# Two heads' retention scores in one run, four grouped heads' values in one run, and a different order at the start, at the first grouped head and at the end of a two-layer trunk

## The reference, cut to what matters

```python
h = x
h = h + _mixer_mla_retention(_rmsnorm(h, ab_norm[i]), ab_w_in[i], ..., ab_w_out[i])   # layer 0
h = h + _swiglu(_rmsnorm(h, ffn_norm[i]), ffn_w_gate[i], ffn_w_up[i], ffn_w_down[i])
h = h + _mixer_swa_stickbreak(_rmsnorm(h, cd_norm[i]), cd_w_in[i], swa_sinks[i], cd_w_out[i])  # layer 1
h = h + _moe(_rmsnorm(h, moe_norm[i]), moe_router[i], moe_w_gate[i], moe_w_up[i], moe_w_down[i])
return _rmsnorm(h, final_norm)

def _rmsnorm(x, g):
    y = xf * lax.rsqrt(jnp.mean(xf * xf, axis=-1, keepdims=True) + EPS)
    return (y * g.astype(jnp.float32)).astype(x.dtype)

# retention, within a block of 128 rows
inner = jnp.einsum('nbqhd,nbkhd->nbhqk', qc, kc) * decay_in[None, None]
out_inner = jnp.einsum('nbhqk,nbkhv->nbqhv', inner, vc)

# one block of the grouped heads
s = jnp.einsum('bqhgd,bkhd->bhgqk', qi, ki, ...) * scale - slopes * dist_f
s = jnp.where(valid, s, -jnp.inf)
m = jnp.maximum(jnp.max(s, axis=-1, keepdims=True), sink)
p = jnp.exp(s - m)
p = p / (jnp.sum(p, axis=-1, keepdims=True) + jnp.exp(sink - m))
return jnp.einsum('bhgqk,bkhd->bqhgd', p.astype(vi.dtype), vi)
```

## Time and profile before

| | us |
|---|---|
| median of 3 runs | 1516.37 |
| lowest and highest run | 1515.61 and 1517.12 |
| the profiled execution, its own time | 1517.4 |
| its span | 1515.5 |
| PE busy | 1501.0 (99%) |
| DVE busy | 1263.5 (83%) |
| ACT busy | 1098.7 (72%) |

### The profile page before, as it was taken

How to read it: one execution, slowest core, us unless ns; L and a number is a source line. 1 busy time by engine, 2 the same in 40 slices (tenths; PEclk the granted TensorE clock), 3 DMA queues, 4 the chain that set the end, 5 groups by cost and what they waited for, 6 DMA issues and landing times.

```text
span 1515.5 us, 22215 instructions
## 1 busy us (share of the span) xinstructions
PE 1501.0 (99%) x7294; PEld 1238.4 (82%) x7294; DVE 1263.5 (83%) x1557; ACT 1098.7 (72%) x1388; POOL 25.8 (2%) x25
## 2 busy tenths in 40 slices
PE   9999999999999999999999999999999999999997
PEld 7778888888877788888888888888888888888885
DVE  5578676666677779999999999999999999999997
ACT  6565555555567757888888788888788788788886
POOL 0000000000000000000000000000000000000000
PEclk9999999999999989999999999999999999999998
DMA  9533374555545459999999999999999999999970
GB/s 339 192 113 128 142 257 167 209 205 195 190 171 178 142 206 398 413 403 394 388 372 386 380 378 376 379 388 368 380 392 367 381 393 360 386 391 358 412 271 30
DMA packets 193224, 454.00 MB, mean 300 GB/s; under 512 B 8176, under 2 KB 12144, under 8 KB 192912
## 3 DMA queue, kind: packets, MB, share of 16 engines
q1 hardware_dynamic: 190560, 443.72, 78.1%
q0 software_dynamic: 2608, 9.57, 2.3%
HBM read 447.37 MB, written 5.90 MB: 299 GB/s over the span
## 4 chain that ended last, share of the span: by engine, by line
PE 97%; DVE 2%; ACT 1%; issue 0%; DVEq 0%; ACTq 0%
PE bank L316 26%; PE bank L318 26%; PE bank L317 26%; PE bank L1515 6%; PE bank L1518 3%; PE bank L2046 1%; PE bank L386 1%; PE bank L818 1%; PE bank L1336 0%; PE bank L1490 0%; PE bank L1327 0%; PE bank L807 0%; PE bank L1811 0%; PE bank L372 0%; DVE w_lo L329 0%; PE bank L2162 0%
## 5 line engine op out<-in xcount | busy, mean ns | idle before, releaser
L329 DVE TENSOR_TENSOR w_lo<-ring_low,w_hi 128x1024 fp32r<-128x1024 f32 (+2 forms) x442 | 532.1, 1216 | 86.8 <-ACT w_hi L325 58.5
L325 ACT ACTIVATE w_hi<-ring_low 128x1024 fp32r<-128x1024 f32 (+2 forms) x442 | 465.5, 1055 | 133.4 <-PE bank L318 126.1
L329 DVE TENSOR_TENSOR w_lo<-ring,w_hi 128x1024 fp32r<-128x1024 f32 x330 | 397.1, 1222 | 35.3 <-ACT w_hi L325 12.4
L325 ACT ACTIVATE w_hi<-ring 128x1024 fp32r<-128x1024 f32 x328 | 346.5, 1061 | 81.0 <-PE bank L318 81.0
L316 PE MATMUL bank<-w_hi,xe_hi 128*128 128x512 f32 x888 | 350.3, 395 | 0.0
L318 PE MATMUL bank<-w_hi,xe_lo 128*128 128x512 f32 x888 | 346.1, 390 | 0.0
L317 PE MATMUL bank<-w_lo,xe_hi 128*128 128x512 f32 x888 | 345.5, 389 | 0.0
L318 PEld LDWEIGHTS bank<-w_hi,xe_lo 128*128 128x128 f32 x888 | 166.7, 188 | 35.4
L317 PEld LDWEIGHTS bank<-w_lo,xe_hi 128*128 128x128 f32 x888 | 166.9, 188 | 33.1
L316 PEld LDWEIGHTS bank<-w_hi,xe_hi 128*128 128x128 f32 x888 | 166.8, 188 | 33.0
L316 PE MATMUL bank<-w_hi,hT_hi 128*128 128x512 f32 x448 | 175.8, 392 | 0.0
(11 more groups left out here) (335 smaller groups left out, 1673.2 us busy)
## 6 DMA issues: line engine op xcount, KB each, us to landing
ring<-m_gate_dram SPq DMA_DIRECT2D x72, 1024.0 KB, 5.4
ring_low<-m_down_dram SPq DMA_DIRECT2D x72, 1024.0 KB, 6.2
ring<-m_up_dram SPq DMA_DIRECT2D x56, 1024.0 KB, 5.4
ring_low<-m_up_dram SPq DMA_DIRECT2D x56, 1024.0 KB, 6.4
ring_low<-m_gate_dram SPq DMA_DIRECT2D x40, 1024.0 KB, 5.7
ring<-m_down_dram SPq DMA_DIRECT2D x40, 1024.0 KB, 6.3
ring_low<-f_gate_dram SPq DMA_DIRECT2D x14, 1024.0 KB, 5.1
ring_low<-f_up_dram SPq DMA_DIRECT2D x14, 1024.0 KB, 6.1
```

The source lines that it names most:

```text
L325: nc.scalar.activation(w_hi[:, buf, 0:width], src, ACT.Copy).then_inc(hi_ready, 1)
L329: nc.vector.tensor_tensor(w_lo[:, buf, 0:width], src, f32(w_hi[:, buf, 0:width]), ALU.subtract).then_inc(split_ready, 1)
```

## The change

Five things are changed; the arithmetic of each result stays the same.

1. **Start.** On ACT the split of unit 4 now stands ahead of the squares, and the squares and the root are spread: block 0 at d = 0, block 1 and the root at d = 1, the wait for `rstd` at d = 2. DVE's reciprocal moves from d = 0 to d = 1, behind its split of unit 4.
2. **Retention scores.** Heads 0 and 1 are issued one behind the other at d = 25, into banks 4 and 7.
3. **First grouped heads.** `scores(0)` (which computes heads 0 and 1) moves from between units 6 and 7 into the middle of unit 7. At d = 8 `exponentials(0)` and `normalised(0)` stand ahead of the split of unit 11 instead of behind it.
4. **Values.** `values` runs four heads at d = 12, 16, 20 and 24, two calls in a row, into the two halves of bank 7. There are four `pT_sb1` buffers instead of two. The mixed parts follow at d = 13, 17, 21 and 25, two pairs each: `mixed_hi(k)` at the start of the step, `mixed_hi(k+1)` behind the weight split and the exponentials, then on DVE `mixed_lo(k)` and `mixed_lo(k+1)` behind `normalised`, both waiting for `mixed_hi(k+1)`.
5. **End.** The last norm works in halves of 512 columns: ACT squares the left halves while DVE still adds the right ones, ACT scales the last block's right half with a product that DVE made ahead, and four DMAs of 256 KB take the place of two of 512 KB.

```diff
-        def sums_of_squares(act, use, by_block):
-            for tb in range(TB):
+        def sums_of_squares(act, use, by_block, blocks=range(TB)):
+            for tb in blocks:
...
+            if TB - 1 not in blocks:
+                return
...
-        def pair_out(bank, v, a):
+        def pair_out(bank, v, a, c0=0):
 
             for first in (True, False):
-                cols, src = (slice(0, 256), slice(0, 256)) if first else (slice(P, 256), slice(256, 384))
+                cols, src = (slice(c0, c0 + 256), slice(0, 256)) if first else (slice(c0 + P, c0 + 256),
+                                                                                slice(256, 384))
...
-        R_BANK = (7, 7, 7, 6, 7, 6, 7, 6)
-        RET_AT = {24: (0,), 25: (1,), 26: (2, 3), 27: (4, 5), 28: (6, 7)}
+        R_BANK = (4, 7, 7, 6, 7, 6, 7, 6)
+        RET_AT = {25: (0, 1), 26: (2, 3), 27: (4, 5), 28: (6, 7)}
...
-                if d + 3 < L0_UNITS:
+                if d + 3 < L0_UNITS and d != 1:
                     l0_hi(act, d + 3)
                 if d == 0:
-                    sums_of_squares(act, 0, False)
+                    l0_hi(act, 4)
+                    sums_of_squares(act, 0, False, (0,))
+                if d == 1:
+                    sums_of_squares(act, 0, False, (1,))
+                if d == 2:
                     act.wait_ge(rstd_done, 1)
...
-                if d == 0:
+                if d == 1:
                     inverse_rms(dve, 0)
...
-                if i:
-                    pe.wait_ge(ret_decayed, {1: 2, 2: 4, 3: 2}.get(i, 2 * i - 2))
+                if i == 0:
+                    pe.wait_ge(nm_done, MLA_H)
+                if i > 1:
+                    pe.wait_ge(ret_decayed, {2: 4, 3: 2}.get(i, 2 * i - 2))
...
             def turned_copy(i):
                 n = MLA_H + i
                 act.wait_ge(pT_banked, n + 1)
-                act.wait_ge(pv_done, n - 1)
-                nc.scalar.activation(pT_sb1[i % 2], pt_bank(i), ACT.Copy).then_inc(pT_done, 1)
+                act.wait_ge(pv_done, n - 3)
+                nc.scalar.activation(pT_sb1[i % 4], pt_bank(i), ACT.Copy).then_inc(pT_done, 1)
 
             def mixed_hi(k):
                 if k < 8:
-                    act.wait_ge(pv_done, MLA_H + 2 * k + 2)
+                    act.wait_ge(pv_done, MLA_H + 4 * (k // 2) + 4)
...
-                if d % 2 and 11 <= d <= 25:
-                    mixed_hi((d - 11) // 2)
+                if d in (13, 17, 21, 25):
+                    mixed_hi((d - 13) // 2)
+                if d == 25:
+                    mixed_hi(7)
...
+                if d == 8:
+                    exponentials(0)
                 if d + 3 < L1_UNITS and d != 1:
                     d_hi(act, d + 3)
...
-                if swa_at(d, 1) is not None and d < 21:
+                if swa_at(d, 1) is not None and 8 < d < 21:
                     exponentials(swa_at(d, 1))
+                if d in (13, 17, 21):
+                    mixed_hi((d - 13) // 2 + 1)
...
             def mixed_lo(k):
-                dve.wait_ge(mixT_hi_done, KM + k + 1)
+                dve.wait_ge(mixT_hi_done, KM + (k | 1 if k < 8 else k) + 1)
...
-                if d % 2 and 11 <= d <= 25:
-                    mixed_lo((d - 11) // 2)
+                if d == 25:
+                    mixed_lo(6)
+                    mixed_lo(7)
...
+                if d == 8:
+                    normalised(0)
                 if d in (22, 23):
                     d_lo(dve, d + 2)
...
-                if swa_at(d, 1) is not None and d < 22:
+                if swa_at(d, 1) is not None and 8 < d < 22:
                     normalised(swa_at(d, 1))
+                if d in (13, 17, 21):
+                    mixed_lo((d - 13) // 2)
+                    mixed_lo((d - 13) // 2 + 1)
...
+                    if (d, kk) == (7, 1):
+                        pe.wait_ge(cT_dve, 2)
+                        scores(0)
...
             def values(i):
                 pe.wait_ge(pT_done, MLA_H + i + 2)
-                if i:
+                if i and i % 4 == 0:
                     pe.wait_ge(mixT_done, KM + i // 2)
...
-                if d == 7:
-                    pe.wait_ge(cT_dve, 2)
...
-                if swa_at(d, 0) is not None and d % 2:
+                if swa_at(d, 0) is not None and d % 2 and d > 7:
                     scores(swa_at(d, 0))
-                if swa_at(d, 3) is not None and d % 2 == 0:
-                    values(swa_at(d, 3))
+                if d in (12, 16, 20, 24):
+                    values(d - 12)
+                    values(d - 10)
...
         def last_root(act, part):
             nc.scalar.preload_act_table(ACT.Sqrt)
             for tb in range(TB):
+                act.wait_ge(sc_done, 4 * part + 5 + tb)
+                nc.scalar.activation(squares[:, tb, :], h[:, tb, 0:512], ACT.Square,
+                                     accum_out=ss_left[:, tb:tb + 1]).then_inc(left_sq, 1)
+            for tb in range(TB):
...
                 act.wait_ge(sc_done, 4 * part + 7 + tb)
-                nc.scalar.activation(squares, h[:, tb, :], ACT.Square, accum_out=ss[:, tb:tb + 1]).then_inc(sq_done, 1)
+                nc.scalar.activation(squares[:, 2 + tb, :], h[:, tb, 512:D], ACT.Square,
+                                     accum_out=ss[:, tb:tb + 1]).then_inc(sq_done, 1)
...
+            nc.scalar.activation(xn[:, 1, 512:D], squares[:, 4, :], ACT.Copy, scale=rstd[:, 1:2]).then_inc(act_scaled, 1)
...
+            nc.vector.tensor_tensor(squares[:, 4, :], h[:, 1, right], fgain[:, right], ALU.mult).then_inc(gained, 1)
+            inverse_root(0)
+            scaled(0, left)
+            inverse_root(1)
+            scaled(0, right)
+            scaled(1, left)
...
+            sp.wait_ge(xn_done, 1)
+            store(0, 0)
+            sp.wait_ge(xn_done, 2)
+            store(0, 1)
+            sp.wait_ge(act_scaled, 1)
+            store(1, 1)
+            sp.wait_ge(xn_done, 3)
+            store(1, 0)
+            sp.wait_ge(out_done, 64)
```

More of the change, by code:

```diff
@@ L166, in trunk @@
         pT_sb1 = [place(f"pT_sb1{i}", [P, 384], at=L1_AT + 24576 + 1536 * i) for i in range(2)]
+        pT_sb1 += [place(f"pT_sb1{i + 2}", [P, 384], at=L1_AT + 37376 + 1536 * i) for i in range(2)]
         bv1 = place("bv1", [P, TB, 512], at=L1_AT + 27648)
@@ L178, in trunk @@
         hT_lo = [place(f"hT_lo{i}", [P, 4, P], F32R, at=(ARENA + 6144, XT_AT + 6144)[i]) for i in range(2)]
-        squares = place("squares", [P, D], at=XT_AT)
+        squares = place("squares", [P, 5, 512], at=XT_AT)
         g_moe_row = place("g_moe_row", [P, D], at=XT_AT + 12288)
@@ L2385, in last_root, with inverse_root, scaled @@
                                      scale=1.0 / D).then_inc(rms_done, 1)
+            act.wait_ge(gained, 1)
+            act.wait_ge(rstd_done, 6)
+            nc.scalar.activation(xn[:, 1, 512:D], squares[:, 4, :], ACT.Copy, scale=rstd[:, 1:2]).then_inc(act_scaled, 1)
         def last_norm(dve):
-            dve.wait_ge(gain_in, 16)
-            for tb in range(TB):
+            def inverse_root(tb):
                 dve.wait_ge(rms_done, 4 + tb + 1)
                 nc.vector.reciprocal(rstd[:, tb:tb + 1], rms[:, tb:tb + 1]).then_inc(rstd_done, 1)
+            def scaled(tb, w):
@@ L2392, in last_norm @@
                 dve.wait_ge(rstd_done, 4 + tb + 1)
-                nc.vector.scalar_tensor_tensor(out=xn[:, tb, :], in0=h[:, tb, :], scalar=rstd[:, tb:tb + 1],
-                                               in1=fgain, op0=ALU.mult, op1=ALU.mult).then_inc(xn_done, 1)
+                nc.vector.scalar_tensor_tensor(out=xn[:, tb, w], in0=h[:, tb, w], scalar=rstd[:, tb:tb + 1],
+                                               in1=fgain[:, w], op0=ALU.mult, op1=ALU.mult).then_inc(xn_done, 1)
+            left, right = slice(0, 512), slice(512, D)
@@ L2489, in _, with store @@
             overflow(sp, moe_sp, moe_sp(sp, 0))
-            for tb in range(TB):
-                sp.wait_ge(xn_done, tb + 1)
-                sp.dma_start(out[0, tb * P:tb * P + P, :], xn[:, tb, :]).then_inc(out_done, 16)
-            sp.wait_ge(out_done, 32)
+            def store(tb, r):
+                w = slice(512 * r, 512 * r + 512)
+                sp.dma_start(out[0, tb * P:tb * P + P, w], xn[:, tb, w]).then_inc(out_done, 16)
+            sp.wait_ge(xn_done, 1)
[7 more added lines that the diff above has]
+            sp.wait_ge(out_done, 64)
         @block.scalar
```

16 lines of the change are left out of this document (13 added, 3 removed).

## The result

| | us |
|---|---|
| kernel before, median of 15 runs | 1516.54 (1515.61 to 1517.70) |
| changed kernel, median of 15 runs | 1520.66 (1518.54 to 1522.28) |
| ratio, 95% interval | 1.0026, 1.0020 to 1.0033 |
| profiled execution of the changed kernel, its span | 1522.11, 1520.3 |

The changed kernel is 4.1 slower (with the interval, 3.0 to 5.0). The page of its profile says as little as that of before: PE is still 99% busy.

What follows compares the result with a forecast made beforehand. PE was taken as the bound (busy 1501.0 of 1515.5), with a 4.03 ACT and DVE chain in grouped-head steps. Gains -2.75, costs +5.7 and clock +1.7 gave +4.65 on 1516.37: 1521.0 us, range 1517.2 to 1522.8.

Steps and rivals of the forecast that it cites:

- start: At the kernel's start, unit 4's earlier split removes PE's 0.53 idle and the refilling of its pipe: -0.75 us.
- retention: At d = 25, retention heads 0 and 1 overlap in different banks, so one head's scores are free: -0.9 us.
- first grouped head: At the first grouped heads, p_sb is ready earlier and the first transpose no longer waits: -0.4 us (0 to -0.45).
- values, steps: At d = 12, 16, 20 second values runs lengthen PE's list; steps losing a run gain nothing: +2.05 us.
- values, d = 24: At d = 24, where PE is already dense, the values run moved there costs its full 0.65 us.
- values, gap at d = 21 and 22: mixed_lo, waiting for the second mixed_hi, delays s_sb on DVE; PE idles 3.9 before transpose 14: +3.0 us (2.6 to 3.3).
- clock behind the gap: After PE's 3.9 gap the clock falls to half speed for some time: +1.7 us, between 0 and 4.
- end: After PE's last matmul, the last norm in halves shortens the path: -0.7 us (-0.2 to -1.2).
- Rival B: The gap comes, but the clock doesn't fall or comes back at once: +2.95, 1519.3 us; chance 0.20.
- Rival D: No gap, and steps at d = 12, 16, 20 absorb the second run: some -3.4, 1513.0 us; chance 0.09.
- C: The gap doesn't come, as mixed_hi or mixed_lo is released earlier than read: 1516.3 us; chance 0.12.
- E: Clock stays low as long as at 546, or the d = 22 delay spreads: +6.5 to +8, 1523 to 1524.5; chance 0.08.

Runs made afterwards that it cites:

- e3: The changed kernel with 18 extra matmuls, results unread, on PE in the gap ahead of transpose 14: 1519.22 us, 2.55 above before.
- e1: The changed kernel with the second mixed_hi of d = 21 moved on ACT ahead of the split of unit 24: 1516.39 us, ratio 1.000.
- e4: The kernel before with the fourth part (values) alone: 1524.28 us, ratio 1.0057.
- e5: The changed kernel with the fourth part (values) undone: 1513.53 us, ratio 0.9981 to before.
- e9b: e5 with two extra matmuls on PE ahead of the wait for x's second half: 1512.99 us, ratio 0.9977 to before.
- e12b: e5 run once more, unchanged, on the same chip as e9b: 1513.73 us, ratio 0.9984 to before.
- e6: e1 with both mixed_lo of d = 21 ahead of normalised(13), and exponentials and normalised ahead of the splits at d = 10, 14, 18: 1514.18 us, ratio 0.9981.
- e7: The kernel before with the first part (start) alone: 1516.69 us, ratio 0.9995.
- e8: e5 with one wait more, retention head 1 waiting until head 0's scores are banked: 1515.65 us, one execution only.

## Why the prediction was right

It gave 1521.0 with 1517.2 to 1522.8 and slower by over 0.2%; the median is 1520.66, +4.1 against the +4.65 of the sum. Term by term, as the prediction put it:

| term | forecast | measured | from |
|---|---|---|---|
| start | -0.75 (-0.4 to -0.8) | -0.9 to -1.1 | 17.54 to 17.76 against 18.68, where the clock stayed up |
| retention | -0.9 | -1.04 | the table of stretches |
| first grouped head | -0.4 | -0.42 | the same |
| values, steps | +2.05 | +1.78 | transpose 0 to 13 |
| values, d = 24 | +0.65 | +0.65 | transpose 15 to the transposes of h |
| values, gap at d = 21 and 22 | +3.0 | +2.96 | transpose 13 to 14 |
| clock behind the gap | +1.7 | +1.65 | transpose 14 to 15, and e3 |
| end | -0.7 | -0.58 | last matmul to the end (in all profiles: 8.1 to 8.6 with the new end, 8.9 to 9.5 with the old) |

With -1.0 for the start the measured terms add up to +4.0, and the medians differ by 4.1.

**The gap** was read from the order of two engines and timed with rows of the kernel before, and this is the term that carried the forecast. Each link of it stands in the timeline above: `mixed_hi` behind the split (forecast for 493.12; transpose 13 comes 1.0 later in this execution, and `mixed_hi` at 494.12), `s_sb` 3.33 behind transpose 13 (forecast 3.2 more than the 0.11 of before), a dense DVE behind it, PE idle for 3.70 (forecast 3.9). e1 shows that the place of the one instruction on ACT is the cause.

**The clock.** The estimate of 1.7 was a choice between 0 and 4, with only the argument that the matmuls behind the gap are dense. That the clock would fall was read rightly from a row: it falls about 1 behind PE's last matmul, and it fell behind a gap of 3.7. That the size came out at 1.65 is luck: nothing in the rows of before said how long a low stretch behind a gap lasts. The Trainium skill, page "TensorE: Matmul & The Clock Gate", section "HAM oscillation — how this bites in real kernels", says that such gaps are paid for by the work behind them, and e3 agrees: without the idleness the same delay costs 1.65 less. Rival B (+2.95, no fall) has its own run in e3, at +2.55 above before; that is about what the changed kernel would have cost had the clock stayed up there.

**The steps.** The mechanism was right: the three steps with two runs take 5.12, 5.12 and 4.66 instead of 4.47, 4.48 and 4.01, and the steps without a run take 4.00 with 0.70 of idle instead of 4.03. Two readings in it were wrong. The prediction took 4.03, which it had read at d = 10, for the steps at d = 12, 16 and 20 too, and so expected about 4.7 with two runs; two of the three were 4.47 and 4.48 already. The term holds all the same, since each grew by the 0.64 to 0.65 of the second run. And it took the busy time for a view in which merging saves 0.6. The busy time fell by 0.6 for other reasons: it is 1502.7 in e4, with the merged values alone, and 1497.4 in e5, with all but these. The term was 0.27 too high: the three steps add 1.94 and not 2.05, and the others give back 0.16 in sum. Rival D (the steps take a second run for nothing) is out: no step did.

**The start** gained more than its bound of 0.8 where x came early. With x at 8.49, as in the profile from which the prediction was worked out, the 9.39 behind it would give 17.88 and a gain of 0.8. It is also the one place where the profile of the changed kernel alone would have misled: it shows the first part as a loss of 0.68, since this execution had the clock fall at 8.4. The prediction has no term for that fall. That it makes much of the spread of the 15 runs (1518.54 to 1522.28), together with the stretch near 550, is likely from e9b and e12b and not shown run by run.

Rivals C and E: the gap came, so C is out; the clock stayed low only 3.4 and the delay did not spread (from transpose 15 to the transposes of h it takes 40.86, as in e1 and e3, whether the gap or the fall is there or not), so E is out. The sum given for D doesn't come out: -2.1 and another 0.5 are -2.6 and 1513.8, not -3.4 and 1513.0, and 1513.8 would not have been clear of the noise. It changes nothing in the forecast itself.

## What to carry to other kernels

Moving a small piece of PE work out of a step gains only if PE bounds that step. Find the chain that bounds the others first: here two weight splits lay on it, and taking them off three steps (e6) gave 1.85, while the merging gave nothing. When an instruction is moved, read what stands behind it on its own engine and behind whoever waits for it; a copy of 0.38 put behind a split of 1.06 cost 4.3 in all (e1). And if PE must wait long, price the clock behind the gap too: filling it with useless matmuls can be the cheaper evil until the wait is mended.

## What the runs showed of the hardware

- In all profiles in which the clock fell behind a gap (the changed kernel near 8 to 12 and near 500, e4, e7, e8, e12b) it was at half (1.2 GHz) for 3.4 and then back at 1.00. Near 500 that cost 1.65 in the changed kernel (6.55 against 4.90) and 1.62 in e4, at the start 1.3 to 1.6. Behind the long gap the fall came when PE was working again: 0.6 after it in the changed kernel, 1.35 in e4.
- Waits of 1.99 to 2.10 on PE at the start were followed by a fall in four of five profiles, and not in e5 (2.08). Waits of 0.78 to 1.76 there never brought one.
- In the routing part, where PE is busy with small matmuls, the half-clock stretch was either 10.2 long (the kernel before, e3, e4) or 6.8 (the eleven others), without any change to that part. From the transposes of h to PE's last matmul it takes 966.0 to 966.1 with the longer one and 964.5 to 965.2 with the shorter. So executions of one kernel differ by 0.8 to 1.6 there, and a part worth less than that can't be read off the medians of a few runs.
